# The prompt's attention in one hybrid decoder step: row blocks in the order 0, 7, 1, 6, 2, 5, 3, 4 instead of 7, 0, 6, 1, 5, 2, 4, 3

## The reference, cut to what matters

```python
def fox_prompt(q, k, v, logf):                 # q, k, v: (1, 1024, 8, 64)
    f_cum = cumsum(logf)                       # per head
    def block(i, q_i, f_i):                    # 128 queries
        sc = q_i @ k.T * scale + (f_i[:, None] - f_cum[None, :])
        sc = where(k_pos <= q_pos, sc, -inf)   # block i sees i + 1 blocks of keys
        return softmax(sc) @ v
    return concat(block(i) for i in range(8))

def fox_sample(q, k, v, logf, k_past, v_past, logf_past):
    s = q @ k_past.T * scale + (f_q - f_cum)   # 4096 past tokens, from the pages
    return softmax([s, s_new]) @ [v_past, v]
```

## Time and profile before

| what | value |
| --- | --- |
| median of three runs | 2725.96 us (2720.02 to 2728.98) |
| the profiled execution's own time | 2720.35 us |
| span of its trace | 2718.4 us |
| PE busy over the span (page) | 2579.7 us (95%) |
| attention stage, first bias to first product of the projection | 356.3 to 614.1 us |
| PE busy in 452 to 492 us, 492 to 548 us, 548 to 612 us | 38.60 of 40, 52.95 of 56, 60.56 of 64 us |

### The profile page before, as it was taken

How to read it: one execution, slowest core, us unless ns; L and a number is a source line. 1 busy time by engine, 2 the same in 40 slices (tenths; PEclk the granted TensorE clock), 3 DMA queues, 4 the chain that set the end, 5 groups by cost and what they waited for, 6 DMA issues and landing times.

```text
span 2718.4 us, 41411 instructions
## 1 busy us (share of the span) xinstructions
PE 2579.7 (95%) x16810; PEld 2459.3 (90%) x16810; DVE 1225.3 (45%) x1491; ACT 669.6 (25%) x942; POOL 885.2 (33%) x554
## 2 busy tenths in 40 slices
PE   5999977999999999999998999879999999999996
PEld 4999954559999999999998999879999999999996
DVE  5988975432533333333336303162533333333335
ACT  4311243542321111111123322221321111111121
POOL 2766641002333333333332212232333333333330
PEclk9999978999999999999999999889999999999998
DMA  3877878983111111111111213312111111111111
GB/s 142 294 279 253 290 274 302 328 291 117 39 47 47 46 46 46 46 46 46 46 53 31 105 42 62 127 51 102 39 48 46 46 46 46 46 46 46 46 42 62
DMA packets 122775, 282.87 MB, mean 104 GB/s; under 512 B 20102, under 2 KB 24071, under 8 KB 122155
## 3 DMA queue, kind: packets, MB, share of 16 engines
q1 hardware_dynamic: 86218, 168.75, 17.6%
q10 hardware_dynamic: 36160, 111.61, 13.5%
q0 software_dynamic: 288, 1.05, 0.1%
HBM read 261.27 MB, written 20.07 MB: 103 GB/s over the span
## 4 chain that ended last, share of the span: by engine, by line
PE 80%; DVE 9%; DMA 3%; issue 3%; ACT 2%; SPq 1%; POOL 1%; POOLq 0%; DVEq 0%; ACTq 0%
PE G L756 68%; PE G L808 2%; DVE KTMP L1884 2%; PE G L846 2%; DMA XT<-in_ck 2%; PE M L969 2%; PE G L1116 1%; DVE XT L1867 1%; SPq L641 1%; PE G L1010 1%; DVE QT L1828 1%; PE M L1061 1%; PE G L1038 1%; DVE KT L1811 1%; DVE XT L1971 1%
## 5 line engine op out<-in xcount | busy, mean ns | idle before, releaser
L2354 POOL TENSOR_TENSOR WLO<-WRAW,WHI 128x1024 fp32r<-128x1024 f32 x192 | 464.7, 2426 | 1286.2 <-ACT WHI L1633 834.1
L756 PE MATMUL G<-HHI,WHI 128*128 128x344 f32 x3312 | 708.4, 322 | 13.7 <-DVE XT L1941 5.1
L756 PE MATMUL G<-HLO,WHI 128*128 128x344 f32 x3312 | 704.8, 321 | 0.0
L756 PE MATMUL G<-HHI,WLO 128*128 128x344 f32 x3312 | 701.1, 320 | 0.0
L756 PEld LDWEIGHTS G<-HHI,WHI 128*128 128x128 f32 x3312 | 558.5, 189 | 17.3 <-issue 14.8
L756 PEld LDWEIGHTS G<-HLO,WHI 128*128 128x128 f32 x3312 | 562.6, 190 | 0.0
L756 PEld LDWEIGHTS G<-HHI,WLO 128*128 128x128 f32 x3312 | 553.7, 188 | 0.0
L2101 DVE TENSOR_TENSOR XT<-XT,G 128x1032 f32<-128x1032 f32 x172 | 211.5, 1230 | 348.8 <-PE G L756 332.8
L1633 ACT ACTIVATE WHI<-WRAW 128x1024 fp32r<-128x1024 f32 x108 | 112.3, 1056 | 494.0 <-PE G L756 494.0
L756 PE MATMUL G<-HIDH,WHI 128*128 128x344 f32 x960 | 204.4, 322 | 0.0
L756 PE MATMUL G<-HIDL,WHI 128*128 128x344 f32 x960 | 202.9, 320 | 0.0
(11 more groups left out here) (332 smaller groups left out, 2769.1 us busy)
## 6 DMA issues: line engine op xcount, KB each, us to landing
WRAW<-in_w ACTq DMA_DIRECT2D x192, 512.0 KB, 3.6
XT<-in_ck SPq DMA_DIRECT2D x256, 256.0 KB, 4.7
HF<-in_cv SPq DMA_DIRECT2D x176, 256.0 KB, 4.8
XT<-in_cv SPq DMA_DIRECT2D x80, 256.0 KB, 4.6
XT<-in_xp SPq DMA_DIRECT2D x2, 4096.0 KB, 16.8
x_scr<-XT SPq DMA_DIRECT2D x1, 4128.0 KB, 12.2
XT<-x_scr SPq DMA_DIRECT2D x1, 4128.0 KB, 13.5
out_y<-XT SPq DMA_DIRECT2D x2, 1376.0 KB, 5.4
```

Of the source, the lines that this page charges most:

```text
L756: mm = pe.matmul(out[:, c], w, x[:, c * TC:(c + 1) * TC], start=first and n == 0, stop=last and n == 2)
L2354: TT(WLO[:, s], WRAW[:, s], WHI[:, s].bitcast(F32), ALU.subtract).then_inc(w_lo, 1)
```

## The change

The order of the blocks within each pair of heads is turned in each neighbouring two: the short block first, then the long one. No instruction is added or taken away, and the same block does the same work. What moves is which step a block falls in, and with it what lies beside it: the first step of a pair holds block 0 instead of 7, and the last one block 4 instead of 3. The tables that are worked out from `BLOCKS` (`ROUNDS`, the count of transposing rounds) follow.

```diff
@@ -187,7 +187,7 @@
-BLOCKS = (7, 0, 6, 1, 5, 2, 4, 3)
+BLOCKS = (0, 7, 1, 6, 2, 5, 3, 4)
```

## The result

The changed kernel takes 2714.36 us (median of 16 runs, 2708.75 to 2721.82), the kernel before 2724.73 us (16 runs, 2718.39 to 2730.69). The ratio is 0.9964, its 95% interval 0.9954 to 0.9973: 9.8 us less, between 7.4 and 12.5. The sum of the prediction gave 0.9962, and the median lies inside its range of 2710.2 to 2724.5.

What follows compares the result with a forecast made beforehand. PE was taken to bound steps 10 to 31, with loads a close second bound. Terms -1.0, -3.75, -3.2, -1.4, -0.4, -0.5 and 0 sum to -10.25 us: 2715.7 us from the median 2725.96, range 2710.2 to 2724.5.

Steps and rivals of the forecast that it cites:

- (a): First pair, steps 0 and 1: block 0 first brings the last key sums and next loads sooner, carried on; -1.0 us.
- (b): Step 8: the load queue is released sooner, so the value PE waits for lands sooner; -3.75 us, bounds -2 and -4.5.
- (d): Third step of a pair: PE's 0.68 us wait behind `pair_high` goes in pairs 1 and 2; -1.4 us, at least 0.
- (e): Pair ends on block 4: its two rounds wait behind bias copies at steps 16 and 24, last steps save; -0.4 us together.
- (c): Second step of a pair: PE's 1.62 us wait for DVE's block 7 scores goes, twice; -3.2 us, a bound is half.
- (f): Pair 3: some low clock and small waits go along with the idle time; -0.5 us, between 0 and -2.
- (g): Stage's end: the longer last block fits in while PE waits for the samples' attention; 0, at most +0.6 us.
- The signs: Traces: release 4.3 us behind step 8's scores, DMA share above 0.03, L1010 waits gone, new L1038 wait, projection near 604 us.
- A: Rival: loads decide the stage's end, so only their earlier start counts; -4.8 us, 2721.2 us, chance 0.18.
- B: Rival: at pair starts block 4's second rounds wait for all ACT has before them; sum -6.9 us, 2719.0, chance 0.10.
- C: Rival: waits move to neighbouring steps and step 8's early release is lost; 0 within 2 us, 2726, chance 0.10.
- D: Rival: PE's clock stays low behind step 8's wait, steps 9 to 15; costs 20 us, about 2736, chance 0.06.

Runs made afterwards that it cites:

- run 5: New block order in pair 0 alone, pairs 1 to 3 as in the kernel before: 2720.86 us, ratio 0.9990 (0.9978 to 1.0002) against the kernel before.
- run 2: New block order in pair 1 alone, other pairs as in the kernel before: 2722.74 us, ratio 0.9998 (0.9986 to 1.0010) against the kernel before.
- run 6: Kernel before with only the first two blocks of each pair exchanged (0, 7, 6, 1, 5, 2, 4, 3): 2713.36 us, ratio 0.9961.
- run 3: Changed kernel, but each pair ends on block 3 instead of 4: 2714.38 us, ratio 0.9970 against the kernel before.
- run 1: New block order in pairs 2 and 3 alone, pairs 0 and 1 as in the kernel before: 2717.46 us, ratio 0.9988 against the kernel before.
- run 7: Changed kernel, with the last key sum also put ahead of step 8's score reduction: 2707.14 us, ratio 0.9943 against the kernel before.
- run 9: Kernel before with each pair's first two blocks exchanged and the last key sum ahead of step 8's scores: 2708.03 us, ratio 0.9951.
- run 4: Kernel before, old order, with the last key sum of step 8 put ahead of the score reduction: 2714.76 us, ratio 0.9970.

## Why the prediction was right in its sum, and where it was not

The total was right, the shares were not, and that the errors made up for each other is luck. Between the marks, the forecast and the traces (first trace of each kernel; the differences of the second pair are within 0.6 us of these but for the first line) stand so:

| stretch | forecast, from | measured |
| --- | --- | --- |
| step 0's scores to step 8's scores | -1.0, (a) | 71.7 to 69.4; over twelve traces 67 to 73 |
| step 8's scores to turning of step 16 | -4.1, (b) (d) (e) | 62.9 to 62.2: -0.7 |
| to turning of step 24 | -2.0, (c) (d) (e) | 55.6 to 54.5: -1.1 |
| to the projection | -3.2, (c) (e) (f) | 62.6 to 57.8: -4.8 |
| sum | -10.25 | 252.8 to 243.9: -8.9; timed -9.8 |

**(a), first pair.** In its place it holds. From the start of step 0's scores to the samples' shift (L2014) it took 9.60 us and takes 8.42 (365.02 to 373.44). Whether this is carried to step 8 can't be seen: that stretch scatters by over 5 us in the twelve traces, whichever order they have, and pair 0 alone has an interval of 6.5 us.

**(b), step 8: the step that failed.** The release, the arrival and the length of the stretch came as said. What failed is the half sentence in brackets: block 7's turning and results move behind the wait, "and equally much comes out further on". It doesn't come out. In the old order PE turned block 7 (2.61 us) while it would have waited for the values anyway. That work was hidden in the wait: PE was busy for 6.67 of the 14.7 us. In the new order only block 0 is there to be turned and PE is busy for 4.60 of 10.9. The 2.1 us that fell out of the wait's shadow stand on the path behind it, and PE's busy time in the stretch up to step 16 rose from 45.09 to 48.75. The other 1.6 us of that rise are not more work, because from step 8's scores to the turning of step 16 both kernels do the same work. They go with the clock: behind the wait 0.89 was granted instead of 0.93, in both traces of each, which over 50 us is worth about 2 us. Why it was lower is not settled; run 5, with the old order in this pair, has 0.91 there. PE's idle time behind the wait fell by 0.6 us, from 3.1 to 2.6. So the stretch reads -3.8 for the wait, +2.1 for the uncovered work, +1.6 for the clock and -0.6 for idle time, which is the -0.7 of the table. Run 2, with the new order in pair 1 alone, needs 0.9 us less for the same stretch. A wait that gets shorter by moving work out of it gains only the difference.

**(c), second step of a pair.** Right: no idle time before the scores of steps 9, 17 and 25, though the cover was thin. Run 6 holds (a), (b) and this term and not the turned end of a pair (e), and it has the whole gain.

**(d), third step.** Half right. The 0.68 us of step 19 are gone, and `pair_high` (L1486) stands behind block 1's exponential as I had said. But in step 18 PE waits 0.77 us, for another copy: `results_high` (L1509) comes right behind block 7's exponential, ahead of the copies of its turned rounds. In the old order it stood behind block 0's exponential, where no two rounds waited for it. The two copies, `results_high` before and `pair_high` after:

```profile
507.29 1.04 ACT L1509 ACTIVATE HHI<-WRAW 128x1024 fp32r<-128x1024 f32 x1
```

```profile
511.38 1.04 ACT L1486 ACTIVATE HHI<-KT 128x1024 fp32r<-128x1024 f32 x1
```

In pair 2 the net is 0.1 us more, and that makes up most of the 0.9 us by which pair 2 fell short. In run 6 neither wait is over 0.25 us, because block 6's longer scores and block 7's longer turning lie before them. Its expectation had `pair_high`'s wait stay, and that was wrong. The term's own bound was 0, and the bad end of the range counted -0.7 for it.

**(e), the block that a pair ends on.** Right: the turning behind the bias copies takes 2.42 us where I had 2.40. Run 3 shows that it evens out: its pairs 1 and 2 need 0.2 and 0.3 us less than those of the changed kernel, and pair 3, which has no pair behind it, 1.6 us more.

**(f), pair 3, mis-sized.** I gave -0.5 to the clock and the small waits and the runs show about -2 (-4.8 in all, less 1.6 of (c) and 1.0 of (e)). The windows below are cut where the results of step 30 end, because from there VectorE's samples' attention sets the time. The first two are of the kernel before, the others of the changed one:

```profile
551.48:608.55 57.07, 53.69 (x510) 32.81 (x510) 22.75 (x74) 24.74 (x58) 0.00 (x0) 0.97 0.82 294
608.55:614.13 5.58, 3.84 (x28) 2.87 (x29) 4.22 (x21) 3.46 (x6) 0.00 (x0) 0.72 0.35 98
```

```profile
551.21:603.37 52.16, 51.05 (x508) 31.83 (x508) 22.61 (x74) 23.31 (x54) 0.00 (x0) 1.00 0.85 309
603.37:608.96 5.59, 3.14 (x35) 2.35 (x34) 4.22 (x21) 3.84 (x8) 0.00 (x0) 1.00 0.38 105
```

The lower clock at the very end costs nothing: the last window is as long at 0.72 as at 1.00. In the first one idle time fell by 2.3 us, 0.7 more than (c), and 57.07 us at 0.97 lack 1.7 us of full clock. The bound of -2 that I had set aside was the better value. How much of it the order brings is open: run 3 has 1.00 in pair 3 too, but runs 1, 6, 7 and 9, which also start it with block 0, have 0.95 to 0.97. Before, a spell at the lower clock begins behind the 1.61 us that PE stands idle in step 25:

```profile
556.00:560.42 4.42, 2.77 (x29) 2.01 (x26) 3.04 (x9) 3.22 (x6) 0.00 (x0) 1.00 1.06 387
560.42:563.83 3.41, 3.41 (x20) 1.75 (x23) 1.45 (x9) 2.68 (x8) 0.00 (x0) 0.50 0.90 328
```

The Trainium skill ("TensorE: Matmul & The Clock Gate", The HAM clock gate) says that the clock is halved after idle time. This pair of rows agrees in the order of events, 1.00 with the idle time in it and 0.50 behind. A spell without idle time before it stands in the last section.

**(g), the end.** Right: from the end of step 30's results to the projection it takes 5.59 us where it took 5.58, so block 4's second round costs nothing.

**The signs.** The release 4.35 us behind the scores, the share of 0.49 and the waits before L1010 came as said; the new wait on L1038 at the start of a pair is 0.74 us (0.58 and 0.16). The projection starts at 608.96 and, in the second trace, 607.12 us and not near 604.

**The rivals.** A fell with run 1, and in the changed kernel no wait of PE for values in pairs 2 and 3 is over 0.31 us. The loads held 387 GB/s from 551 to 580 us in the changed kernel, with PE busy for 28.30 of 28.80 us. In pair 1 of the kernel before, the single slices stand between 300 and 389 and not between 330 and 370 as I had read them, which leaves the argument as it is. The row of the changed kernel:

```profile
551.20:580.00 28.80, 28.30 (x273) 16.29 (x272) 13.78 (x46) 14.46 (x34) 0.00 (x0) 1.00 1.05 387
```

The Trainium skill's page "HBM Reference" (Specifications) adds to the 358 GB/s that I had cited that a core which streams alone measures well above its share; the row agrees. B fell with run 3. C was right about one place, pair 1, and wrong about the kernel. D did not come: the stretch behind the wait in step 8, its place, has the lower clock of (b), worth about 2 us and not 20 or more. PE's busy time over the span rose by 3.1 us (2579.7 before, 2582.8), but not in the stage: from step 0's scores to the projection it fell from 219.4 to 216.6 us, and it rose in the parts before and behind, which have the same instructions in both kernels.

**What stays open.** The three parts by themselves (runs 1, 2 and 5) add up to 6.5 us and the whole gives 9.8. The intervals overlap, and the trace of run 1 has a lack of 1.7 us: in it the first values of step 24 fell into a spell at the lower clock that the changed kernel doesn't have there. Run 2 has the spell in pair 2 told above. The timeline of run 1:

```profile
549.10 3.60 PE L969 MATMUL M<-HF,SCR 128*32 128x512 f32 x16
```

and that of the changed kernel:

```profile
551.21 1.92 PE L969 MATMUL M<-HF,SCR 128*32 128x512 f32 x16
```

The same 16 matmuls take 1.68 us more. What puts the spell there I did not settle. Nor did I settle how much of the 9.8 us is (a).

## What to carry to other kernels

Before counting a shorter wait as a gain, list the work that runs inside it: what the edit moves out of the wait's shadow must be paid elsewhere. Here an edit that released earlier without moving work (run 4) gained 8.2 us, and one that moved work (run 2) 0.5. Putting a short block at each place where an engine must wait for the block before it, as in the first two steps of a pair, gave here all that the full reordering gave. When parts of a sum are checked, check them between marks of the work: the right total of 9.8 us hid one stretch that I had forecast 3.4 us too large and another 1.6 us too small.

## What the runs showed of the hardware

The lower level of PE's clock (1.2 GHz) came at the start of a pair also without idle time before it. In run 4 PE went through the bias products of 8 rows (L990, from 482.51 us) and one round of turning with no wait, and then the values came at half the clock; in the same trace a second spell lies behind the 1.62 us of idle time in step 17. The windows of run 4 over the two:

```profile
485.69:489.10 3.41, 3.41 (x16) 0.48 (x16) 0.00 (x0) 0.97 (x2) 0.00 (x0) 0.50 0.97 348
495.94:499.35 3.41, 3.37 (x17) 1.97 (x20) 0.85 (x7) 2.54 (x9) 0.00 (x0) 0.50 0.02 5
```

Where PE is the bound such a spell costs up to half its length, 1.7 us. Run 1 has one at the start of pair 3 and the changed kernel, with the same order there, doesn't, so it belongs into the range of any forecast here, at 1.7 us a time.

Outside the stage, between the start of the projection and the end, nothing differs between the kernels, and yet the twelve traces lie between 2101.7 and 2108.4 us; the scores of step 0 start anywhere from 359.8 to 365.0 us. This is why single executions can't settle terms of 1 to 3 us when they are compared by their spans.
